# Two-block transformer forward on one Trainium2 core: the modulation's gates summed by four transposes and a row sum, then spread over partitions through DRAM

## The reference, cut to what matters

```python
mod = jax.nn.silu(c) @ w_ada + b_ada            # c: 1 x 1024, w_ada: 1024 x 9216
sh1, sc1, g1, sh2, sc2, g2, sh3, sc3, g3 = [m[:, None, :] for m in jnp.split(mod, N_MOD, axis=-1)]
u = rms_norm(x, ffn1_norm_g) * (1 + sc1) + sh1
x = x + 0.5 * g1 * swiglu(u, ffn1_w_in, ffn1_w_out)
u = rms_norm(x, mix_norm_g) * (1 + sc2) + sh2
...                                             # the mixing part, ending in merged
x = x + g2 * (merged @ w_out)
u = rms_norm(x, ffn2_norm_g) * (1 + sc3) + sh3
x = x + 0.5 * g3 * swiglu(u, ffn2_w_in, ffn2_w_out)
```

## Time and profile before

| What | Value |
|---|---|
| time, three runs | 992.17, 993.47, 994.43 us |
| profiled execution, first to last instruction | 994.2 us (the page gives no other time of its own for it) |
| TensorE (PE) busy | 98% of the span |
| VectorE (DVE) busy | 72% |
| ScalarE (ACT) busy | 53% |
| DMA engines, mean | 216 GB/s |
| granted TensorE clock, mean | 0.995 |

### The profile page before, as it was taken

The page is one execution under the profiler, slowest core; times in us unless marked ns, Lnnn a source line. Parts: engine busy times, 40 slices in busy tenths (PEclk is TensorE's granted clock), DMA queues, the critical chain, the costliest instruction groups (busy, mean ns, idle before and its releaser), DMA issues.

```text
span 994.2 us, 12848 instructions
## 1 busy us (share of the span) xinstructions
PE 975.9 (98%) x4770; PEld 806.2 (81%) x4770; DVE 715.9 (72%) x1074; ACT 522.4 (53%) x808; POOL 58.4 (6%) x62
## 2 busy tenths in 40 slices
PE   8999999999999999999999999999999999999998
PEld 6878788888887888888878888877888878888886
DVE  5867778886786767767869988686667766566653
ACT  6576565554346444444467645567454474443531
POOL 3310100000000000000000022021000000000000
PEclk9998999999999999999999999999999999999999
DMA  7940667888795777778756766865565737664761
GB/s 245 300 132 1 222 221 226 279 271 274 264 316 192 254 262 246 247 251 325 262 149 208 229 210 190 288 194 175 150 199 199 236 111 222 215 209 134 253 225 51
DMA packets 116444, 214.64 MB, mean 216 GB/s; under 512 B 9058, under 2 KB 16506, under 8 KB 116126
## 3 DMA queue, kind: packets, MB, share of 16 engines
q1 hardware_dynamic: 116238, 213.73, 65.7%
q10 hardware_dynamic: 144, 0.10, 0.0%
HBM read 212.71 MB, written 2.13 MB: 216 GB/s over the span
## 4 chain that ended last, share of the span: by engine, by line
PE 89%; DVE 5%; DMA 2%; ACT 2%; issue 1%; POOL 0%; SPq 0%; ACTq 0%; DVEq 0%
PE ps L1179 27%; PE ps L1181 26%; PE ps L1180 26%; PE ps L1229 3%; PE ps L1316 2%; DVE wlo L1846 2%; PE ps L1271 1%; PE ps L1297 1%; PE ps L1207 1%; ACT whi L1484 1%; DMA raw<-in_w_up 1%; DMA raw<-in_w_in 1%; DMA araw<-in_w_ada 1%; DMA raw<-in_ffn_w_in 1%; PE ps L1367 1%
## 5 line engine op out<-in xcount | busy, mean ns | idle before, releaser
L1484 ACT ACTIVATE whi<-raw 128x1024 fp32r<-128x1024 f32 (+2 forms) x307 | 313.0, 1028 | 282.4 <-PE ps L1181 193.0
L1846 DVE TENSOR_TENSOR wlo<-raw,whi 128x1024 fp32r<-128x1024 f32 (+2 forms) x307 | 358.3, 1189 | 49.0 <-ACT whi L1484 48.2
L1179 PE MATMUL ps<-whi,hTh 128*128 128x512 f32 (+1 forms) x832 | 326.2, 392 | 2.7 <-DVE wlo L1846 2.7
L1181 PE MATMUL ps<-whi,hTl 128*128 128x512 f32 (+1 forms) x832 | 316.5, 380 | 0.0
L1180 PE MATMUL ps<-wlo,hTh 128*128 128x512 f32 (+1 forms) x832 | 316.4, 380 | 0.0
L1179 PEld LDWEIGHTS ps<-whi,hTh 128*128 128x128 f32 x832 | 156.8, 188 | 33.6 <-DVE wlo L1846 3.8
L1181 PEld LDWEIGHTS ps<-whi,hTl 128*128 128x128 f32 x832 | 156.7, 188 | 30.8
L1180 PEld LDWEIGHTS ps<-wlo,hTh 128*128 128x128 f32 x832 | 157.0, 189 | 26.9 <-issue 0.2
L2188 DVE SCALAR_TENSOR_TENSOR aacc<-araw,cs,aacc 128x512 f32<-128x512 f32 x126 | 94.4, 749 | 4.8 <-DMA araw<-in_w_ada 2.2
L2430 POOL TENSOR_TENSOR stat<-stat,mhalf 128x8 f32<-128x8 f32 (+3 forms) x29 | 38.3, 1331 | 632.3 <-DVE stat L1862 486.3
L1179 PE MATMUL ps<-whi,uh_ffn 128*128 128x512 f32 x176 | 69.8, 396 | 0.0
(11 more groups left out here) (251 smaller groups left out, 1092.0 us busy)
## 6 DMA issues: line engine op xcount, KB each, us to landing
raw<-in_ffn_w_in SPq DMA_DIRECT2D x80, 512.0 KB, 4.5
araw<-in_w_ada SPq DMA_DIRECT2D x72, 512.0 KB, 4.9
raw<-in_w_mix SPq DMA_DIRECT2D x64, 512.0 KB, 4.4
raw<-in_ffn_w_out SPq DMA_DIRECT2D x44, 512.0 KB, 4.9
raw<-in_w_up SPq DMA_DIRECT2D x32, 512.0 KB, 4.9
raw<-in_w_down SPq DMA_DIRECT2D x32, 512.0 KB, 5.2
raw<-in_w_out SPq DMA_DIRECT2D x16, 512.0 KB, 4.2
raw<-in_w_in SPq DMA_DIRECT2D x12, 512.0 KB, 5.6
```

The lines of the kernel that those rows point to most:

```text
L1179: pe.e.matmul(o, ah, h[:, j, :], start=s0, stop=False, skip_group_check=True)
L1181: r = pe.e.matmul(o, al, h[:, j, :], start=False, stop=s1, skip_group_check=True)
L1484: act.e.activation(uflat(whi, u), uflat(raw, u), ACT.Copy).then_inc(hi.up(u), 1)
L1846: v.tensor_tensor(uflat(wlo, u), uflat(raw, u), uflat(whi, u).bitcast(f32), SUB).then_inc(lo_dve.up(u), 1)
```

## The change

All 18 blocks are now summed in the same way: four transposes on PE, a row sum and a bias from the column table on DVE, into `modc`. For the parts m = 2 and 8 DVE halves the four columns. For the six gate blocks SP then stores the 128 x 4 columns as one row of 512 values to a new DRAM scratch `scrM`, waits for the store, and loads that row into all 128 partitions of `gates`. The residuals wait for that load (`gate_loaded`) and not for DVE. The row loads of `b_ada` are gone. In the plan a gate block has two more steps behind its sum step: one for the store and one for the load; its name goes into `done` behind the second. The number of steps rises from 91 to 103 (ACT's count of them is raised to match), and the sum step of block j is step 6 + 5j + 2 x (gate blocks before j).

```diff
+    scrM = nc.dram_tensor("scr_m", (6, 512), f32, kind="Internal").ap()
+    st_mod = signal("st_mod", 16)
+    ld_gate = [signal(f"ld_gate{i}", 16) for i in range(2)]
...  plan, ada()
-                    if h == 3 and m % 3 == 2:
-                        rowr.take("ada", j)
...
                 if m % 3 == 2:
-                    rowr.drop("ada", j)
+                    for _ in range(2):
+                        yield
+                        seg("ada")
                 done.add(("ada", j))
                 yield
...
+    def is_gate(j):
+        return j // 2 % 3 == 2
+
+    def gate_loaded(m):
+        return ld_gate[m // 3 % 2](m, 1)
...  tensor_program, ada()
-                if j // 2 % 3 < 2:
-                    for q in range(4):
-                        r = pe.e.transpose(bank[:, q * 128:(q + 1) * 128], acc[:, q * 128:(q + 1) * 128], ident[:, :])
-                else:
-                    r = pe.e.matmul(bank[:, :], ones[:, 0:128], acc[:, :], start=True, stop=True)
+                for q in range(4):
+                    r = pe.e.transpose(bank[:, q * 128:(q + 1) * 128], acc[:, q * 128:(q + 1) * 128], ident[:, :])
...
-                yield
+                for _ in range(3 if is_gate(j) else 1):
+                    yield
...  vector_program, residual()
-                dve.wait_ge(*mod({"mix": 5, "ffn2": 11, "end": 17}[stage]))
+                dve.wait_ge(*gate_loaded({"mix": 2, "ffn2": 5, "end": 8}[stage]))
...  vector_program, ada()
+                r = v.tensor_tensor(modc[:, c0:c0 + 4], modc[:, c0:c0 + 4], col("bada", c0, 4), ADD)
+                if m in (2, 8):
+                    step(r)
                     dve.wait_ge(*dve_step.now())
-                    v.tensor_tensor(modc[:, c0:c0 + 4], modc[:, c0:c0 + 4], col("bada", c0, 4), ADD).then_inc(mod.up(j), 1)
-                else:
-                    g = gates[m // 3 % 2][:, j % 2 * 512:(j % 2 + 1) * 512]
-                    dve.wait_ge(*ld_row[rowr.at("ada", j)]("ada", j))
...
-                    r = v.tensor_tensor(g, bank[:, :], rowr.buf("ada", j)[:, :], ADD)
...
-                        v.tensor_scalar(g, g, 0.5, None, MUL).then_inc(mod.up(j), 1)
+                    r = v.tensor_scalar(modc[:, c0:c0 + 4], modc[:, c0:c0 + 4], 0.5, None, MUL)
+                r.then_inc(mod.up(j), 1)
...  sync_program, ada()
+            def gate_store(j):
+                c0, row = j // 2 * 8 + j % 2 * 4, j // 6 * 2 + j % 2
+                sp.wait_ge(*mod(j))
+                q.dma_start(bass.AP(scrM.tensor, row * 512, [[1, 128], [128, 4]]), modc[:, c0:c0 + 4],
+                            allow_slow_non_contiguous=True).then_inc(st_mod.up(j), 16)
+
+            def gate_load(j):
+                m, c, row = j // 2, j % 2, j // 6 * 2 + j % 2
+                sp.wait_ge(*st_mod(j))
+                if m == 8:
+                    sp.wait_ge(*gated("mix", 1, c))
+                q.dma_start(gates[m // 3 % 2][:, c * 512:(c + 1) * 512], rows(scrM, row * 512, [[1, 512]])).then_inc(
+                    ld_gate[m // 3 % 2].up(m, c), 16)
...
-                    if h == 3 and j // 2 % 3 == 2:
-                        load_row(d["b_ada"], j * 512, "ada", j)
                     yield
                 yield
+                if is_gate(j):
+                    gate_store(j)
+                    yield
+                    gate_load(j)
+                    yield
```

More of the change, by code:

```diff
@@ L1689, in ada @@
             act.e.activation(cs[:, :], col("c", 0, 8), ACT.Silu).then_inc(c_silu.up(), 1)
-            for _ in range(91):
+            for _ in range(1 + 18 * 5 + 6 * 2):
                 yield
@@ L2193, in ada @@
                 dve.wait_ge(*ada_sum(j))
[L2194 to L2198, removed]
-                    dve.wait_ge(*dve_step.now())
-                    v.tensor_tensor(modc[:, c0:c0 + 4], modc[:, c0:c0 + 4], col("bada", c0, 4), ADD).then_inc(mod.up(j), 1)
-                else:
-                    g = gates[m // 3 % 2][:, j % 2 * 512:(j % 2 + 1) * 512]
-                    dve.wait_ge(*ld_row[rowr.at("ada", j)]("ada", j))
-                    if m == 8:
-                        dve.wait_ge(*gated("mix", 1, 1))
-                    r = v.tensor_tensor(g, bank[:, :], rowr.buf("ada", j)[:, :], ADD)
[L2207 to L2215, removed]
-                        v.tensor_scalar(g, g, 0.5, None, MUL).then_inc(mod.up(j), 1)
-                yield
+                c0 = m * 8 + j % 2 * 4
+                dve.wait_ge(*ld_c())
+                step(v.tensor_reduce(modc[:, c0:c0 + 4], heads(bank[:, :], 4), AX, ADD))
+                misc.give(dve_step.now(), "ada", j)
+                dve.wait_ge(*dve_step.now())
+                r = v.tensor_tensor(modc[:, c0:c0 + 4], modc[:, c0:c0 + 4], col("bada", c0, 4), ADD)
+                if m in (2, 8):
+                    step(r)
+                    dve.wait_ge(*dve_step.now())
+                    r = v.tensor_scalar(modc[:, c0:c0 + 4], modc[:, c0:c0 + 4], 0.5, None, MUL)
+                r.then_inc(mod.up(j), 1)
+                for _ in range(3 if is_gate(j) else 1):
+                    yield
         def up_job(name, c):
@@ L2709 @@
     given = {"x": "x", "w_in": "w_in", "w_out": "w_out", "w_up": "w_up", "w_down": "w_down", "w_ada": "w_ada_2",
-             "b_ada": "b_ada_2", "ffn1_w_in": "ffn1_w_in_2", "ffn1_w_out": "ffn1_w_out_2", "w_mix": "w_mix_2",
+             "ffn1_w_in": "ffn1_w_in_2", "ffn1_w_out": "ffn1_w_out_2", "w_mix": "w_mix_2",
              "b_mix": "b_mix_2", "mlstm_norm_g": "mlstm_norm_g_2",
```

## The result

The changed kernel takes 1033.66 us (median of four runs, 1030.75 to 1034.35) against 993.95 us before (now a median of four runs too): ratio 1.0388, 95% interval 1.0371 to 1.0404. It is slower by 39.7 us. Forecast were 1017.6 us and at most 1024: the direction was right, the size was not.

What follows compares the result with a forecast made beforehand. PE was taken as the bound, busy for 98% of the span. -2.5 + 13.4 + 8.5 + 0.7 + 4.0 = 24.1 us on a profiled span of 994.2 us gave a predicted 1017.6 us, range 1009 to 1024.

Steps and rivals of the forecast that it cites:

- PE's own part: At six gate blocks, transposes (0.44 us) replace products with ones (0.86 us): 2.5 us less, ends 0 and 3.
- SP's own part: Six stores and two waits in SP's queue: holds of about 4 us are covered, so 0 us, ends 0 and 3.
- The forecast's own sign of being wrong: Unit loads waiting behind SP's wait for a store would make the prediction wrong; SP should wait only in the second bunch.
- The landing: A gate store's landing in DRAM was taken as 1.6 us after issue, upper end some 8 us.
- The cover: ACT needs a queued unit load only when PE is four units (11 us) short, so SP's 4 us hold is covered.
- The second rival: Scattered stores take 8 us each, holding SP 4 us at four blocks, 8 at the last: 3 to 8 us, chance 0.07.
- The count of steps: Extra steps force steps 83 to 89 ahead of the mixing tail and 99 to 103 ahead of ffn2's output product.
- The first bunch: Seven steps back to back ahead of the mixing part's tail: PE waits, costing 13.4 us, 11.8 to 15.4.
- The rivals that it would be hidden or half covered: Back-to-back steps run under PE's halves, 991.0 us, chance 0.05; or are partly absorbed, 1003 to 1009 us, chance 0.10.
- The second bunch: Five steps back to back ahead of ffn2's output product: PE waits 8.5 us, ends 7.7 and 9.5.
- The clock: PE drops to 1.2 GHz behind each of the two long waits: 2 x 2.0 = 4.0 us, ends 2 and 6.8.
- Small shifts: In the convolution's stretch a step call holds a chunk instead of a sum: +0.7 us, ends 0 and 1.

Runs made afterwards that it cites:

- e9_extra: e7_rows with one more product with ones, overwritten afterwards, in each of the 18 sum steps: 1008.83 us, ratio 1.0145 to before.
- e5_16byte: The changed kernel with each store written as 128 pieces of 16 bytes, which permutes the gates' columns: 1018.43 us, ratio 1.0240 to before.
- e1_steps: The kernel before with two empty steps behind the sum of each gate block, nothing else of the change: 1021.65 us, ratio 1.0270 to before.
- e3_late: The changed kernel without the extra steps (91 steps), each gate row's load four steps behind its store: 1005.28 us, ratio 1.0107 to before.
- e7_rows: e3_late with the columns transposed on PE and stored as four rows of 512 bytes, load two steps behind: 993.05 us, measured again 993.73 us.
- e2_holds: The changed kernel without the extra steps (91 steps), each gate row's load one step behind its store: 1010.90 us, ratio 1.0155 to before.
- e10_rate: e1_steps with denser step calls, every 8 halves for 13 in the mixing part and 6 for 10 in ffn2: 995.88 us, ratio 1.0009 to before.
- e6_warm: e1_steps with 11 and 9 pairs of useless products keeping PE busy while it waits for DVE's accumulation: 1017.50 us, ratio 1.0232 to before.

## Why the prediction was right or wrong

**PE's own part, -2.5 us: not settled.** A product does cost 0.84 to 0.88 us (e9_extra). Six fewer with six more groups of transposes should give 2.5 us, of which the small transposes for the stores take back up to 0.7. The measured gain is 1.4 and 1.2 us by the medians of two rounds, with intervals that hold both 0 and 1.8. A second reading leans towards the forecast: e5_16byte has the steps of e1_steps and the cheaper sums, and is 3.2 us faster (1.0240 for 1.0270), with a store that is not free; those intervals too overlap by a hair.

**SP's own part, 0 us with ends 0 and 3: this is the step that failed.** It failed at three points, and the runs price them together at 15.2 us (changed kernel against e5_16byte). The forecast's own sign of being wrong came with it: SP waited for a store at five of six, and unit loads behind it.

- The landing. The nearest row was a store of whole rows, 1.6 us, and the upper end was set at 8 us. It was 9.0 to 11.8. The Trainium skill (DMA: Bandwidth & Descriptors, "Rules for kernel authors") spoke against the store: it says that a last dimension which isn't contiguous is lowered to one descriptor for each element. The trace agrees, with 3168 small packets more for 3072 elements, and a quarter of the pieces landed in half the time (4.6 us for 9.5). I had kept to the row of another kind of store. An upper end from a transfer of 512 KB was no bound for 512 pieces.
- The engines. I asked only who waits for the store, which is SP. The larger part is that the transfers behind it come late, also those of another queue: 12.2 us by e3_late against e7_rows, in a kernel without the extra steps.
- The cover. It was worked out for unit loads in mid-stage, and in the changed kernel the 12.6 us were indeed lost at the two tails, where the norm's chain needs the next units at once. Block 11's store and load fell on the last steps ahead of the mixing tail; my own count of steps put them there (68 and 69), and I didn't look what followed. Block 5's store stood five steps ahead of ffn1's tail, and a unit load of 9.39 us behind it is in that chain. Nor is mid-stage safe: `araw` loads queue behind SP too, and in e2_holds one of them cost PE a wait of 6.7 us there.

The second rival, slow scattered stores, named the right mechanism with a chance of 0.07, a hold of 4 us at four blocks and 3 to 8 us in all. The sign was right and the size half of it, since it knew only the hold.

**The count of steps: right.** Seven steps were forced ahead of the mixing tail and five ahead of ffn2's output product. e1_steps shows that they act alone, e10_rate that they cost nothing when spread.

**The first bunch, 13.4 + 2.0 us: right.** Measured 15.1. DVE's order in the trace is the predicted one, chunk by chunk. Landings were 4.5, 4.5 and 3.6 us for the 4.4 taken. The rivals that it would be hidden or half covered fall.

**The second bunch, 8.5 + 2.0 us less 0.8 for two sums: a little low.** 9.7 predicted, 10.8 measured. PE's wait was 9.1 us, as the last chunk's load took 5.2 us and not 4.4, and the half clock lasted into 971 us.

**The clock, 4.0 us: right within what can be measured.** One minus the clock, summed over the windows from 810 to 815 and from 966 to 972 us, is 2.1 and 2.6 us, so 4.7 in all; e6_warm against e1_steps gives 4.2. Not foreseen were two more such stretches, at the two tails; their cost is in the 12.6 us.

**Small shifts, 0.7 us: right.** 0.5 in the convolution.

The sum without the store was 24.1 us; e5_16byte, the change with a cheap store, stands 24 us above before. That the two agree to 0.1 us is luck: the second bunch alone was off by 1.1, and four runs tell no better than about 1 us. All but about 1 us of the error is the store. A wider range would not have helped: the sum's own upper end, +36.7, gives 1030 us, still under 1033.66, as it held 3 us for SP where 15 were needed.

## What to carry to other kernels

Ask of a new transfer how many pieces it has, not only how many bytes and who waits for it: here the loads behind it paid, whichever of two queues the store was on. Turning a 128 x 4 tile once on TensorE, 0.27 us, took away all that could be measured of the cost of six such stores.

Where side work is fed in by a counter and caught up by force at deadlines, adding a step anywhere moves all that follows; count to the next deadlines before anything else. And the last units ahead of a norm are a bad place for a wait on the queue that loads them, as is any place where a load with only two buffers stands behind it.

## What the runs showed of the hardware that was not expected

- 2 KB stored as 512 pieces of four bytes land after 9.0 to 11.8 us; as 128 pieces of 16 bytes after 1.4 to 5.5 us. Loads of 512 KB that e3_late issues behind the first kind take 11.5 to 12.4 us, where the median of its unit loads is 4.6.
- Putting the store on GpSimd's queue does not help: its landing was 9.5 to 11.6 us, and the loads that SP issued behind it took up to 11.95 us. The page counts 192 small packets more for it and 3168 for SP's, at the same time: its count of packets is no measure of this price.
- PE's idle time has a second price: behind waits of 10.7 and 9.1 us it ran at 1.2 GHz for some 3.5 and 5 us more. Filling the waits with useless matmuls gave back about 4 us.
- Two profiled executions of one kernel differed by 7.7 us in span, with mean clocks of 1.000 and 0.991. In this kernel, bound by PE, the time goes with the clock: of its 24 runs the four with a mean clock of 1.000 took 989.68 to 992.17 us and the four at 0.993 or below 995.60 to 998.22 us.
